# Transposed feed-forward projections and identity products in the inverse of a fused two-layer kernel

## The reference

```python
# gated_delta_rule: 32 heads, chunks of 64 in the reference; for every head
sol = triangular_solve(L + I, rhs, lower=True, unit_diagonal=True)

# swiglu: w_gu is 2048 x 11264, w_down is 5632 x 2048
gate, up = jnp.split(h @ w_gu, 2, axis=-1)
return (jax.nn.silu(gate) * up) @ w_down
```

## Time and profile before

| | us |
|---|---|
| median of 3 runs | 2956.25 (2954.28 to 2958.66) |
| the profiled execution | 2955.76 |
| its span, first to last instruction | 2953.8 |
| TensorE busy | 2831.6 (96%) |
| VectorE busy | 1907.2 (65%) |
| ScalarE busy | 1206.1 (41%) |
| GpSimd busy | 813.1 (28%) |
| mean granted TensorE clock | 0.969 |

### The profile page before, as it was taken

How to read it: one execution, slowest core, us unless ns; L and a number is a source line. 1 busy time by engine, 2 the same in 40 slices (tenths; PEclk the granted TensorE clock), 3 DMA queues, 4 the chain that set the end, 5 groups by cost and what they waited for, 6 DMA issues and landing times.

```text
span 2953.8 us, 55253 instructions
## 1 busy us (share of the span) xinstructions
PE 2831.6 (96%) x22110; PEld 2578.7 (87%) x22110; DVE 1907.2 (65%) x2314; ACT 1206.1 (41%) x1511; POOL 813.1 (28%) x554
## 2 busy tenths in 40 slices
PE   6999999999999999999999999969999999999998
PEld 4788988888887788999999999959988989999996
DVE  1376766765765757765666666686889888654454
ACT  2355355355355344433333333344333333533343
POOL 1065665665666630000000000000655553000000
PEclk8999999999999899999999999989999999999999
DMA  9855655655655656655565555636454454565564
GB/s 364 303 170 201 205 174 193 208 187 181 210 186 171 200 179 192 201 188 186 184 187 185 185 189 187 184 106 182 141 159 150 149 165 150 182 187 183 182 201 148
DMA packets 283928, 552.86 MB, mean 187 GB/s; under 512 B 16817, under 2 KB 54258, under 8 KB 282610
## 3 DMA queue, kind: packets, MB, share of 16 engines
q1 hardware_dynamic: 263632, 474.02, 50.9%
q0 software_dynamic: 19408, 76.06, 6.9%
q10 hardware_dynamic: 722, 0.28, 0.0%
HBM read 548.19 MB, written 2.10 MB: 186 GB/s over the span
## 4 chain that ended last, share of the span: by engine, by line
PE 84%; DVE 10%; issue 2%; DMA 2%; ACT 2%; DVEq 0%; POOL 0%; SPq 0%; ACTq 0%; POOLq 0%; PEld 0%
PE pg L1087 32%; PE pg L816 13%; PE pd L1100 11%; PE pd L1087 7%; PE pg L807 5%; PE pg L1100 3%; PE pg L837 2%; PE pd L731 2%; DVE wl L1982 2%; DMA arena<-in_mod_w 1%; PE pd L958 1%; PE pd L972 1%; PE pd L987 1%; PE pd L957 1%; DVE arena L2261 1%
## 5 line engine op out<-in xcount | busy, mean ns | idle before, releaser
L1982 DVE TENSOR_TENSOR wl<-wr,wh 128x1024 fp32r<-128x1024 f32 x616 | 768.0, 1257 | 552.4 <-ACT wh L1529 551.0
L1529 ACT ACTIVATE wh<-wr 128x1024 fp32r<-128x1024 f32 x616 | 652.3, 1060 | 1031.2 <-PE pg L1087 660.4
L1087 PE MATMUL pg<-hh,wh 128*128 128x256 f32 x2944 | 838.7, 285 | 17.9 <-issue 7.7
L1087 PE MATMUL pg<-hl,wh 128*128 128x256 f32 x2944 | 834.7, 284 | 0.0
L1087 PE MATMUL pg<-hh,wl 128*128 128x256 f32 x2944 | 834.1, 283 | 0.0
L588 POOL TENSOR_TENSOR wl<-wr,wh 128x1024 fp32r<-128x1024 f32 x195 | 476.8, 2449 | 474.4 <-ACT wh L1347 474.1
L1087 PEld LDWEIGHTS pg<-hh,wh 128*128 128x128 f32 x2944 | 566.0, 192 | 32.1 <-issue 21.0
L1087 PEld LDWEIGHTS pg<-hl,wh 128*128 128x128 f32 x2944 | 565.9, 192 | 0.5
L1087 PEld LDWEIGHTS pg<-hh,wl 128*128 128x128 f32 x2944 | 566.2, 192 | 0.0
L1347 ACT ACTIVATE wh<-wr 128x1024 fp32r<-128x1024 f32 x216 | 226.9, 1056 | 406.1 <-PE pg L816 240.2
L816 PE MATMUL pg<-hh,wh 128*128 128x256 f32 x1024 | 308.1, 301 | 1.1 <-ACT arena L1395 1.1
(11 more groups left out here) (381 smaller groups left out, 4691.3 us busy)
## 6 DMA issues: line engine op xcount, KB each, us to landing
wr<-in_w_in SPq DMA_DIRECT2D x224, 512.0 KB, 4.1
wr<-in_ffn_w_gu SPq DMA_DIRECT2D x176, 512.0 KB, 3.6
wr<-in_gdn_w_in SPq DMA_DIRECT2D x128, 512.0 KB, 4.2
arena<-in_mod_w POOLq DMA_DIRECT2D x64, 1024.0 KB, 6.7
wr<-in_ffn_w_down SPq DMA_DIRECT2D x88, 512.0 KB, 4.6
arena<-in_mod_w SPq DMA_DIRECT2D x32, 1024.0 KB, 12.2
wr<-in_gdn_w_in SPq DMA_DIRECT2D x128, 256.0 KB, 2.9
wr<-in_gdn_w_out SPq DMA_DIRECT2D x56, 512.0 KB, 4.6
```

Source lines behind the costliest of these rows:

```text
L1087: m = nc.tensor.matmul(bank[:, n * T:(n + 1) * T], w[s][:, k, n * P:(n + 1) * P], act[x][:, k0 + k, :], skip_group_check=True, start=(firs ...
L1529: a(wh[c % 4][:], wraw[c % 4], ACT.Copy).then_inc(s_hc, 1)
L1982: v.tensor_tensor(wl[c % 4][:], wraw[c % 4], wh[c % 4][:].bitcast(F32), ALU.subtract).then_inc(s_lc, 1)
```

## The change

In the inverse, `flip_blocks` made the transposes of the lower partitions (rows 0 to 63) with TensorE's transpose (L957) and those of rows 64 to 127 as a product with the identity (L958). Now both are products with the identity. In the feed-forward block the gate and up projections use `tgroup` in place of `group`: the activations are stationary, and the weights move. Their results, and so `hgt`, have tokens on partitions, while the down projection needs channels there. `hidden_flip` on TensorE therefore transposes `hgt` with eight 128x128 transposes into `pd[0]`, ahead of the fourth gate chunk of the next pass (and, for the last round, ahead of its down projection). DVE's `hidden` keeps only the product; a new `hidden_parts` does the split from `pd[0]`, in the loop after step 3 of `stream`.

```diff
                 def flip_blocks(bank, src, at):
                     for n in range(8):
-                        nc.tensor.transpose(block(bank, 0, slot(n)), src[0:64, at(n), :], ident[0:64, 0:64])
-                        m = nc.tensor.matmul(block(bank, 1, slot(n)), src[64:P, at(n), :], ident[64:P, 64:P], start=True, stop=True)
+                        for b in range(2):
+                            r = slice(64 * b, 64 * b + 64)
+                            m = nc.tensor.matmul(block(bank, b, slot(n)), src[r, at(n), :], ident[r, r],
+                                                 start=True, stop=True)
...
+            def hidden_flip(it):
+
+                pe.wait_ge(s_hm, it + 1)
+                pe.wait_ge(s_dn, it * 4 + 1)
+                for k in range(4):
+                    for h in range(TT):
+                        m = tr(pd[0][:, k * T + h * P:k * T + (h + 1) * P], halves(fl(hgt))[:, h, k * P:(k + 1) * P])
+                m.then_inc(s_ht, 1)
+
+            def gate_chunk(j, t):
+                if t == 3:
+                    hidden_flip(j)
+
+            tgroup(0, 0, CK_FF, pg[0], h_s, 8, lambda t: pe.wait_ge(s_hn, 1 + t // 2))
+            tgroup(0, 0, CK_FF + 8, pg[1], h_s, 8)
             with pe.Fori(0, KF // 4 - 1) as j:
                 pe.wait_ge(s_sg, j + 1)
-                group(j, 24, CK_FB, pg[0], h_s, 8)
+                tgroup(j, 24, CK_FB, pg[0], h_s, 8, lambda t: gate_chunk(j, t))
                 down(j, 24, CK_FB + 8, j)
                 pe.wait_ge(s_hm, j + 1)
-                group(j, 24, CK_FB + 16, pg[1], h_s, 8)
+                tgroup(j, 24, CK_FB + 16, pg[1], h_s, 8)
+            hidden_flip(KF // 4 - 1)
             down(0, 0, CK_FD, KF // 4 - 1)
...
                 v.tensor_tensor(fl(hgt), fl(sg), pg[1][:], ALU.mult).then_inc(s_hm, 1)
-                dve.wait_ge(s_hm, it + 1)
-                parts(hg_s, slice(0, 4), hgt).then_inc(s_hg, 1)
+
+            def hidden_parts(it):
+
+                restart()
+                dve.wait_ge(s_ht, it + 1)
+                link(v.tensor_copy(fl(hg_s[0][:]), pd[0][:]))
+                v.tensor_tensor(fl(hg_s[1][:]), pd[0][:], fl(hg_s[0][:]).bitcast(F32), ALU.subtract).then_inc(s_hg, 1)
...
-                stream(j, 24, CK_FB, 24, {**{9 + 2 * n: (lambda n=n: down(j, 24, CK_FB + 9 + 2 * n, n))
+                stream(j, 24, CK_FB, 24, {3: lambda: hidden_parts(j), **{9 + 2 * n: (lambda n=n: down(j, 24, CK_FB + 9 + 2 * n, n))
                                              for n in range(4)}, 23: lambda: hidden(j, 24, CK_FB + 23, j + 1)})
...
+            hidden_parts(KF // 4 - 1)
             stream(0, 0, CK_FD, 8, {1 + 2 * n: (lambda n=n: down_last(n)) for n in range(4)})
```

More of the change, by code:

```diff
@@ L328, in heads, with fl @@
             return x.rearrange("p (m a) t -> p m a t", a=2)
+        def fl(x):
+            return x.rearrange("p a b -> p (a b)")
         def halves(bank):
@@ L393, in build @@
         s_hm = sem("s_hm")
+        s_ht = sem("s_ht")
         s_dn = sem("s_dn")
@@ L1195, in down @@
                     tgroup(j, per, c + 2 * n, pd[n % 2], hg_s, 2)
-            group(0, 0, CK_FF, pg[0], h_s, 8, lambda t: pe.wait_ge(s_hn, 1 + t // 2))
-            group(0, 0, CK_FF + 8, pg[1], h_s, 8)
+            def hidden_flip(it):
[10 more added lines that the diff above has]
+            tgroup(0, 0, CK_FF + 8, pg[1], h_s, 8)
             with pe.Fori(0, KF // 4 - 1) as j:
                 pe.wait_ge(s_sg, j + 1)
-                group(j, 24, CK_FB, pg[0], h_s, 8)
+                tgroup(j, 24, CK_FB, pg[0], h_s, 8, lambda t: gate_chunk(j, t))
                 down(j, 24, CK_FB + 8, j)
                 pe.wait_ge(s_hm, j + 1)
-                group(j, 24, CK_FB + 16, pg[1], h_s, 8)
+                tgroup(j, 24, CK_FB + 16, pg[1], h_s, 8)
+            hidden_flip(KF // 4 - 1)
             down(0, 0, CK_FD, KF // 4 - 1)
@@ L1522, in turn @@
                 silu_z(j + 1)
-            fl = lambda x: x.rearrange("p a b -> p (a b)")
             def high(j, per, c):
```

## The result

| | before | after |
|---|---|---|
| median of the runs, us | 2956.38 (4 runs, 2954.28 to 2958.66) | 2886.89 (4 runs, 2883.14 to 2888.58) |
| ratio | | 0.9763, 95% interval 0.9746 to 0.978 |
| profiled execution, us | 2955.76 | 2888.58 |
| its span, us | 2953.8 | 2886.6 |

What follows compares the result with a forecast made beforehand. TensorE was taken to bound the kernel; 37.3 us from the sets, 23.2 from the clock and 9.1 from the feed-forward block sum to 69.6 off 2955.76, forecast 2886 us, range 2868 to 2912 (8 in 10).

Steps and rivals of the forecast that it cites:

- The bound: Whole kernel: TensorE bounds it, busy for 96% of the span and holding 84% of the chain.
- The sets: Inverse, 16 sets of 64x64 flips, two per iteration: 3.43 us each falls to 1.08, together 37.3 us saved.
- The clock: Chunks behind the inverse's sets: TensorE's granted clock no longer falls there, 23.2 us saved; lower bound 0.
- The first rival: Behind the inverse's sets: the clock still falls, so the time is 2909 us without the 23.2; chance 15%.
- The fourth rival: Inverse sets: identity products keep 0.26 us each, as between transposes, so the kernel is slower, 2966 us; chance 4%.
- The feed-forward chunks: 176 gate and up chunks: 2.863 us each falls to 2.753 in the new orientation, 19.4 us saved.
- The third rival: Feed-forward block: chunks gain only 0.03 us each, so it costs 5.0 us instead of bringing 9.1, 2900 us; chance 5%.
- The last round: Last down projection: TensorE's uncovered wait of 3.39 us becomes 5.0 with the new transposes and split, 1.6 us lost.
- What stays uncovered in the inverse: Steps behind the sets: ACT, DVE and POOL keep up with the earlier TensorE; charged nothing.
- the second rival: Inverse: DVE's queue makes TensorE wait 1.5 us for each of 16 sets, 24 us, giving 2910; chance 10%.
- The upside that was held at 0: End of each inverse iteration: one more clock fall might vanish too, up to 11 us saved; counted as 0.

Runs made afterwards that it cites:

- fourfold set: Kernel before the change, its sets made identity products and each issued four times over (64 products): 2941.30 us, ratio 0.9938.
- second profile: The changed kernel, unaltered, measured and profiled once more: 2887.16 us, ratio 0.9759; profiled span 2884.7 us.
- woven kernel: Changed kernel with each iteration's second set issued pair by pair together with the eight products that follow it: 2880.40 us, ratio 0.974.
- grouped sets: Kernel before the change with each set reordered, first its eight transposes, then its eight products: 2905.13 us, ratio 0.9814.
- the halves: Changed kernel with each set's eight products of rows 0 to 63 first, then the eight of rows 64 to 127: 2901.85 us, ratio 0.9802.

## Why the prediction was right

**The bound.** TensorE's list was the bound, and shortening it shortened the kernel. Right.

**The sets.** I took 1.08 us from L972, and the sets have 1.08. I took 2.15 for a second set with its eight products; it is 1.83, since the ends of the two overlap. That is 8 x 0.32 = 2.6 us more gained. In the first iteration the set brought 3.2 where 2.7 was charged, and the last iteration's first set 3.0 for 2.8. The sets come to 40.7 us against the 37.3 of the sum.

**The clock.** The lower bound of this term was 0, and the full value came: no fall behind 15 of the 16 sets, and 24.2 us less in the chunks behind them against the 23.2 of the sum. The first rival is refuted. But the reason that I gave was half wrong. I laid the falls to 3.4 us of nothing but small products and transposes. The fourfold set is 3.88 us of small products with no fall. The falls came with the long alternating sets; what in them counts is open.

**The fourth rival and the page.** I argued against the section "Transposes" of the Trainium skill's page "Perfetto Trace Analysis" that a transpose costs 0.18 us of a pair, more than twice a product. That reading was wrong, though the conclusion held. The 0.18 was the change of kind. Grouped, a 64x64 transpose costs 0.07 us and a product in one block 0.13: a transpose is the cheaper of the two, which agrees with the section's advice. Sixteen alternating products beat eight transposes and eight products (1.08 against 1.63) because the two halves overlap. No run has sixteen transposes, so what a set of transposes alone would take is open.

**The feed-forward chunks.** 2.753 predicted, 2.757 measured; a pass 66.9 and 66.96. By the rule in "Back-to-back issue gap" of the Trainium skill's page "TensorE: Matmul & The Clock Gate" only 5 us would have come; the trace disagrees, since 2.863 to 2.757 over 176 chunks is 18.7 us. The section itself calls that gap the isolated one and gives about 131 ns for 512 columns in a stream with loads; the trace has 229. The third rival falls.

**The last round.** The waits were sized right (5.0, measured 5.07). The term left out is the clock that falls behind the longer wait, 1.4 us. Predicted -9.1 for the block, measured -7.2.

**What stays uncovered in the inverse.** I charged nothing, and in the first seven iterations no new wait of TensorE appeared behind the sets. In the last one it did: behind its first set TensorE now waits for DVE twice, where L987 and L731 before had no wait.

```profile
956.80 0.69 PE L993 MATMUL pd<-arena 64*64 64x64 f32 x32 [0.94 <-DVE arena L1921]
960.99 0.33 PE L735 MATMUL pd<-ident,arena 128*128 128x128 f32 x1 [0.53 <-DVE arena L1926]
```

The way from that set's chunk to the second set is 40.26 us against 38.62, so 1.6 us of the gain are given back (in the second profile these waits come to 3.7 us). This is the second rival's mechanism, at a small part of the 24 us that it put on it. In this profile 1.8 us on the other side hide it: ahead of the first iteration's first set TensorE waited 1.72 us for DVE before, and behind the late start of this execution it does not. The second profile has that wait again. So the inverse gained 65.3 us here against the 60.5 of the sum, and 63.1 in the second profile.

**The upside that was held at 0.** The fall at an iteration's end is gone in three of the seven iterations that had it, and I put up to 11 us on all seven. Those three are worth nothing. The stretch from L1050 (now L1056) to the second chunk behind it, before and after:

```profile
277.79:289.35 11.56, 10.81 (x58) 8.24 (x56) 6.05 (x9) 9.99 (x12) 8.13 (x6) 0.85 0.59 191
```

```profile
274.01:285.59 11.58, 9.61 (x57) 6.85 (x55) 9.36 (x9) 10.62 (x12) 8.18 (x6) 1.00 0.60 193
```

11.56 us at a clock of 0.85, and 11.58 at 1.00. The changed kernel has both kinds side by side, here in its second and third iteration:

```profile
375.30:386.94 11.64, 10.89 (x58) 8.32 (x56) 6.51 (x9) 9.99 (x12) 8.14 (x6) 0.85 0.59 189
476.63:488.23 11.60, 9.62 (x57) 6.85 (x55) 9.38 (x9) 10.63 (x12) 8.20 (x6) 1.00 0.60 190
```

With the faster clock TensorE only waits longer for DVE:

```profile
281.77 0.70 PE L912 MATMUL pd<-arena,ones 128*128 128x512 f32 x1 [1.22 <-DVE arena L1881]
```

**What cancelled.** 4.8 us more from the inverse and 1.7 from the rest stand against 7.0 lost at the start, which was in no term, and 1.9 less from the feed-forward block. So the sum hit closer (2886.2 and 2888.6 for the profiled execution) than its terms did, and that part is luck. Neither the start nor the rest repeats: in the second profile the start is 0.75 us later than before and not 7.0, and the rest 988.1 us, not shorter than the 987.6 before. There the inverse and the feed-forward block bring 63.1 + 7.2 = 70.3 us, against the 69.6 of the sum.

## What to carry to other kernels

Price a sequence of small TensorE instructions by the distance between starts, and compare a mixed sequence with a uniform one before calling either kind dear: the changes between transposes and products of 64x64 cost more than both together (1.8 us of 3.43). Group by kind, and let products in different blocks of the array take turns: two blocks here, three in the woven kernel. A fall of the granted clock is worth its price only where TensorE, and not the engine that it waits for next, sets the end of the stretch.

## What the runs showed of the hardware

The start of the program has two forms, in code that no kernel here changed. In the changed kernel's first profile DVE's square (L1881) and a POOL product (L625) begin at the same moment, 171.59 us:

```profile
171.59 2.97 DVE L1881 TENSOR_TENSOR arena<-arena 128x1024 f32<-128x1024 f32 x1 [1.12 <-ACT arena L1421]
```

```profile
171.59 1.88 POOL L625 TENSOR_TENSOR arena<-arena,ident 32x1024 f32<-32x1024 f32 x1
```

In the kernel before, the same two instructions, 40 ns apart:

```profile
172.19 1.22 DVE L1862 TENSOR_TENSOR arena<-arena 128x1024 f32<-128x1024 f32 x1 [1.13 <-ACT arena L1401]
```

```profile
172.23 2.93 POOL L621 TENSOR_TENSOR arena<-arena,ident 32x1024 f32<-32x1024 f32 x1
```

One of the two runs at its own speed and the other takes longer, by 1.75 us on DVE or 1.05 on POOL. In the twelve profiles it is the one that begins later. In nine DVE begins 12 to 37 ns first, and POOL takes 2.93 to 2.96 us; in the other three (this one, the grouped sets and the halves) POOL begins 1, 136 and 29 ns first, and DVE takes 2.97, 2.83 and 2.94. When it is DVE, TensorE waits 3.2 us, its clock falls (7.42 us at 0.50 follow) and the first Gram products begin 7 us later:

```profile
174.61:182.03 7.42, 7.42 (x8) 2.33 (x8) 4.03 (x5) 3.55 (x4) 2.74 (x2) 0.50 0.97 341
```

The second profile of the changed kernel has the short form (1.23 us on DVE, Gram products at 187.64 us), and the grouped sets, which are the kernel before in all else, have the long one. So the form is not the change's doing. Which runs had which cannot be told without their profiles; the medians of the two measurements, 2886.89 and 2887.16 us, agree.
